# A decoder trunk step: placing the turned rope queries after the finish, not before it, in VectorE's queue

## The reference

```python
def mla_project(xn, pos, w_down, g_q_lora, w_uq, g_kv_lora, g_qn, g_qr, g_kr):
    b, t = xn.shape[:2]
    d = xn @ w_down
    cq = rmsnorm(d[..., :Q_LORA], g_q_lora)
    ...
    q = (cq @ w_uq).reshape(b, t, N_HEADS, QK_NOPE + QK_ROPE)
    cos, sin = rope_cos_sin(pos)
    q_nope = rmsnorm(q[..., :QK_NOPE], g_qn)
    q_rope = apply_rope(rmsnorm(q[..., QK_NOPE:], g_qr), cos[:, None], sin[:, None])
    ...
```

## Time and profile before

| | us |
|---|---|
| median of 3 runs (lowest to highest) | 1959.62 (1959.49 to 1959.9) |
| the profiled execution | 1959.83 |
| its span in the trace | 1958.0 |
| TensorE matmul busy | 1922.3 (98%) |
| VectorE busy | 1073.7 (55%) |
| ScalarE busy | 758.4 (39%) |
| GpSimd busy | 702.9 (36%) |

### The profile page before, as it was taken

One profiled execution on the slowest core, in us unless ns is written; L12 is line 12 of the kernel. 1 busy time (PEld: TensorE's weight loads), 2 busy tenths in 40 slices (PEclk: granted clock), 3 DMA queues, 4 the chain that ended last, 5 costly groups with the idle time before them and its releaser, 6 DMA issues.

```text
span 1958.0 us, 36321 instructions
## 1 busy us (share of the span) xinstructions
PE 1922.3 (98%) x13285; PEld 1845.1 (94%) x13285; DVE 1073.7 (55%) x1844; ACT 758.4 (39%) x1508; POOL 702.9 (36%) x690
## 2 busy tenths in 40 slices
PE   7999999999999999999999999999999999999999
PEld 7886669999999999999999999999889999999998
DVE  3787655565556555468535425428864852542541
ACT  4555555554555555332112112247653211221221
POOL 3340003422223233443333333366545343333331
PEclk9999999999999999999999999999999999999999
DMA  5321001111111110222322322332222222223223
GB/s 148 65 65 36 25 13 43 38 31 50 36 35 34 44 40 16 75 77 85 86 78 84 86 80 81 86 100 73 76 67 83 79 82 86 81 80 86 85 76 91
DMA packets 253078, 131.47 MB, mean 67 GB/s; under 512 B 43073, under 2 KB 250754, under 8 KB 252882
## 3 DMA queue, kind: packets, MB, share of 16 engines
q1 hardware_dynamic: 252514, 128.56, 23.5%
q10 hardware_dynamic: 444, 1.29, 0.2%
HBM read 126.21 MB, written 3.61 MB: 66 GB/s over the span
## 4 chain that ended last, share of the span: by engine, by line
PE 87%; DVE 9%; ACT 2%; issue 2%; DMA 0%; DVEq 0%; POOL 0%; SPq 0%; ACTq 0%; POOLq 0%
PE ps L200 18%; PE ps L203 18%; PE ps L201 18%; PE ps L1220 7%; PE ps L1218 7%; PE ps L1219 7%; PE ps L1248 3%; PE ps L1023 2%; PE ps L998 2%; PE ps L1185 2%; DVE arena L1856 1%; PE ps L232 1%; PE ps L1014 1%; DVE arena L2112 1%; DVE split L1859 1%
## 5 line engine op out<-in xcount | busy, mean ns | idle before, releaser
L200 PE MATMUL ps<-split,whi 128*128 128x288 f32 x3024 | 888.5, 296 | 10.9 <-DVE split L273 4.2
L201 PE MATMUL ps<-split,whi 128*128 128x288 f32 x3024 | 884.8, 295 | 0.0
L203 PE MATMUL ps<-split,wlo 128*128 128x288 f32 x3024 | 855.5, 295 | 0.0
L194 POOL TENSOR_TENSOR wlo<-raw,whi 128x1024 fp32r<-128x1024 f32 x187 | 455.6, 2438 | 614.2 <-ACT whi L171 613.8
L200 PEld LDWEIGHTS ps<-split,whi 128*128 128x128 f32 x3024 | 568.5, 188 | 14.6 <-issue 13.0
L201 PEld LDWEIGHTS ps<-split,whi 128*128 128x128 f32 x3024 | 568.5, 188 | 0.4
L203 PEld LDWEIGHTS ps<-split,wlo 128*128 128x128 f32 x3024 | 555.8, 188 | 0.0
L171 ACT CAST whi<-raw 128x1024 fp32r<-128x1024 f32 x187 | 194.8, 1043 | 373.6 <-DMA raw<-in_ffn_w_up 226.6
L1218 PE MATMUL ps<-split,split 128*128 128x384 f32 x768 | 268.2, 349 | 0.0
L1468 DVE TENSOR_REDUCE ssq<-arena 128x16 f32<-128x1024 f32 x128 | 156.1, 1220 | 186.6 <-ACT arena L1330 186.6
L1220 PE MATMUL ps<-split,split 128*128 128x384 f32 x768 | 257.9, 336 | 0.0
(11 more groups left out here) (282 smaller groups left out, 2095.3 us busy)
## 6 DMA issues: line engine op xcount, KB each, us to landing
raw<-in_ffn_w_up SPq DMA_DIRECT2D x96, 512.0 KB, 3.8
raw<-in_ffn_w_down SPq DMA_DIRECT2D x48, 512.0 KB, 3.9
arena<-in_cache_ckv SPq DMA_DIRECT2D x128, 128.0 KB, 2.0
raw<-in_rec_w_in SPq DMA_DIRECT2D x16, 512.0 KB, 3.9
raw<-in_attn_w_o SPq DMA_DIRECT2D x8, 512.0 KB, 3.9
raw<-in_rec_w_out SPq DMA_DIRECT2D x8, 512.0 KB, 4.1
raw<-in_attn_w_down SPq DMA_DIRECT2D x7, 512.0 KB, 7.6
raw<-in_attn_w_uq SPq DMA_DIRECT2D x48, 64.0 KB, 2.2
```

What stands on the lines that cost most here:

```text
L194: pool.tensor_tensor(wlo[:, t % RING, :], raw[:, t % RING, :], f32(whi[:, t % RING, :]), ALU.subtract).then_inc(w_lo, 1)
L200: pe.matmul(o, wh, a, start=first, stop=False)
L201: pe.matmul(o, wh, b, start=False, stop=False)
L203: mm = pe.matmul(o, wl, a, start=False, stop=last)
```

## The change

In `uq_dve` the call of `uq_place` moves from behind the evacuation to the end of the turn, so that it follows the finish of group p-1.

```diff
@@ -798,8 +798,6 @@
                 uq_evacuate(dve, p)
                 if p == 1:
                     rope_key_turned(dve)
-                if p - 3 in ROPES[:-1]:
-                    uq_place(dve, p - 3)
                 if p == 0:
                     rope_key(dve)
                     down_low(dve, 4)
@@ -810,6 +808,8 @@
                     uq_finish(dve, p - 1)
                 if p - 2 in ROPES:
                     uq_sin(dve, p - 2)
+                if p - 3 in ROPES[:-1]:
+                    uq_place(dve, p - 3)
```

## The result

The changed kernel takes 1975.14 us (median of 4 runs, 1972.96 to 1975.63), against 1959.76 us before on the same chip. The ratio is 1.0073 with a 95% interval of 1.0062 to 1.0085, so it is slower by 12 to 17 us. In the comparisons further down two executions ran at a lower granted clock throughout (one of the kernel before, 2350.82 us at 0.752, and one of turn7, 2060.19 us at 0.946); ratios and intervals leave them out, and the medians move by under 0.2 us with them. The forecast was 1971.8 us in a range of 1964.5 to 1976.0. The profiled execution took 1975.19 us, its span is 1973.3: 15.3 us above the span before.

What follows compares the result with a forecast made beforehand. The prediction took TensorE to bound the kernel (87% of the chain), VectorE's order mattering only where TensorE waits for it. Its terms 2.1 + 7.3 + 1.6 + 1.2 = +12.2 us gave a median of 1971.8 us, range 1964.5 to 1976.0.

Steps and rivals of the forecast that it cites:

- Turn 4, +2.1: Query projection, turn 4: finish(3) waits for the Exp, evacuation(5) and product(6) come 2.1 us later; TensorE stalls 3.0 us.
- Turn 7, rotation earlier, sum(8) +1.5 with a stall of 3.1: Turn 7: rotation(6) starts 1.6 us earlier, but evacuation(8) 1.7 later; sum(8), held by sine(6), starts 1.5 later.
- Turn 9, +7.3 with the 1.5 of turn 8: Turn 9: placement(6) meets two GpSimd subtractions, delaying evacuation(10); product(11) starts 7.3 us later, sum(8)'s 1.5 included.
- The stall of 5.6 us before product(11): Turn 9: TensorE has nothing to do from about 128.8 and stands 5.6 us until product(11).
- The clock, 1.6 + 1.2 = 2.8: Lower granted clock behind stalls: +1.6 us behind the 5.6 us stall, +1.2 for one of the two shorter ones.
- The coin for the two shorter stalls: Stalls of 3.0 and 3.1 us: even odds each of lowering the clock, costing 1.4 or about 1.0; one counted.
- the most for one drop: Limit for one clock drop, from the trace before: 3.9 us of work at half speed cost 1.9 us.
- rival (d): Forecast with other clock outcomes: no stall lowers it, 1969; all do, 1973.5; longer low clock, up to 1976; no separate chance.
- The shift behind the stage: Turns 10 and 11, the value stage and later loads shift rigidly; DMAs cost nothing, a late one a microsecond or two.
- (a): Rival, turn 9: placement(6) does not meet the subtractions, product(11) +2.9 instead of 7.3; +6.2, 1965.8 us; 8%.
- (b): Rival, not slower: finishing earlier pays, rotation(6) 1.6 us earlier, evacuations not delayed; 1958.0 us; 7% in all.
- (c): Rival: only turn 4's +2.1 stays, turns 7 to 9 hide in TensorE's products; 1961.7 us, no change; 5%.

Runs made afterwards that it cites:

- turn7: Kernel before with only placement(4) moved behind finish(6), in turn 7; 1963.46 us, ratio 1.0016.
- sine_first: Changed kernel with sine(6) put ahead of finish(7) in turn 8; 1972.80 us, ratio 1.0059.
- pool_after: Changed kernel with GpSimd waiting for placement(6) before the low parts of the value weights; 1966.85 us, ratio 1.0031.
- turn9_pool: Kernel before with only placement(6) moved behind finish(8), and GpSimd waiting for it before the value weights' low parts; 1962.50 us, ratio 1.0010.
- warm3: Changed kernel with 6, 6 and 9 extra unread matmuls on TensorE ahead of product(6), sum(8) and product(11); 1969.49 us, ratio 1.0048.
- pool_early: Kernel before with GpSimd waiting for finish(3) before the low part of one weight tile, in turn 4; 1960.35 us, ratio 0.9996.
- turn4: Kernel before with only placement(1) moved behind finish(3), in turn 4; 1964.65 us, ratio 1.0021.

## Why the prediction was right, and which term was too small

**Turn 4, +2.1.** Right. The finish waited 2.06 us (2.0 predicted), the placement ended 101.59, and evacuation(5) comes 9.68 us behind evacuation(4) (91.94 to 101.62) instead of 7.65 (92.29 to 99.94): +2.0. TensorE's stall was 3.00 us, the 3.0 of the text.

**Turn 7, rotation earlier, sum(8) +1.5 with a stall of 3.1.** Right in each step. Evacuation(8) came 8.40 us behind evacuation(7) (112.62 to 121.02), before 6.75 (109.38 to 116.13): +1.65 for the 1.7. The stall was 3.06. That the sine holds sum(8) is shown by sine_first.

**Turn 9, +7.3 with the 1.5 of turn 8.** Right as a mechanism: placement(6) lasted 7.20 us for the "about 7.5" (133.45 - 126.0) of the text, and pool_after and turn9_pool show that GpSimd's two subtractions stretch it. Together with turn 4 the sum had 9.4, and warm3, the kernel without the clock's part, measured 9.2. Evacuation(10) stands at 137.65, 2.0 us behind the 135.6 that the prediction gave without any clock cost. That is the clock's 1.6 us of product(6) and 1.1 of sum(8), below, less a start that is 0.35 earlier and a placement 0.25 shorter.

**The stall of 5.6 us before product(11)** was 3.65. Sum(8), the transposes and product(10) ran slow behind the stall before sum(8) and filled the rest; sum(9) was at 132.90, 7.8 us behind sum(8) in place of 5.1. The prediction had said that product(10)'s slowness has slack, and had not carried it into the length of the next stall.

**The clock, 1.6 + 1.2 = 2.8.** This is the term that was too small: 5.3 us in the stage. The coin for the two shorter stalls was counted once, and both fell: product(6) cost 4.79 - 3.23 = 1.6 us (1.4 said), sum(8) 1.1 (1.0 said). Behind the stall of 3.65 us the low level lasted through all of product(11), 5.90 - 3.24 = 2.7 us for the 1.6 taken and beyond the 1.9 that was called the most for one drop. The three add up to 5.4, the 5.3 of the comparison with warm3. That it is the clock, and not something else slow on TensorE, is shown by warm3.

The step that set the 1.9 was a reading of the first drop in the trace before. The prediction took the 3.9 us from the stall's end at 19.10 to about 23.0 for what one drop can cost. But the clock had fallen inside that stall; the windows from which this is seen stand ahead of those in the earlier trace rows:

```profile
16.00:18.00 2.00, 0.00 (x0) 0.00 (x0) 1.30 (x4) 1.21 (x2) 2.00 (x4) 0.54 1.09 320
18.00:20.00 2.00, 0.90 (x4) 0.93 (x5) 2.00 (x3) 2.00 (x4) 0.34 (x1) 0.50 1.19 268
```

At 0.54 on average in 16 to 18 it was low from about 16.2, so for 6.8 us in all, of which 2.9 fell into the stall and cost nothing. Behind product(11)'s stall it was low for 6.8 us as well (137.7 to 144.5), but only 0.9 of them, up to 138.55, lay in the stall. The low stretch was no longer than the one before; more of it lay under work.

With all clock outcomes at their bound the prediction's own sum was 2.1 + 7.3 + 4.8 = 14.2, 1974.0 us against the profiled execution's 1959.83. The result of 1975.14 lies above that. It is in the range only because rival (d) had put the upper end at 1976, for a low level longer than either row shows, and no row gave that figure. The mechanism of each place was right; that the range held was in part luck.

**The shift behind the stage.** Predicted as rigid; 1.2 us were added, and they come from one place near the end. The trace before has its second drop at 1418 to 1422 us and none at 1440 to 1444, where TensorE waited 2.7 us for VectorE's L2157. After, the same wait is 3.0 us, 13.8 us later, and behind it the clock is low. Two windows behind the wait, before and, under it, after:

```profile
1442.00:1444.00 2.00, 2.00 (x18) 1.95 (x17) 0.00 (x0) 0.00 (x0) 1.57 (x1) 1.00 0.00 0
```

```profile
1456.00:1458.00 2.00, 2.00 (x11) 2.00 (x10) 0.00 (x0) 0.00 (x0) 1.33 (x1) 0.50 0.00 0
```

VectorE's last row ahead of L2157 and its next row behind it, which waits for TensorE, before and, under it, after:

```profile
1438.68 0.75 DVE L2153 TENSOR_TENSOR arena<-arena 128x576 f32<-128x576 f32 x1
...
1444.77 1.22 DVE L2210 COPY arena<-ps 36x1024 f32<-36x1024 f32 x1 [3.77 <-PE ps L2205]
```

```profile
1452.48 0.75 DVE L2153 TENSOR_TENSOR arena<-arena 128x576 f32<-128x576 f32 x1
...
1460.15 1.22 DVE L2210 COPY arena<-ps 36x1024 f32<-36x1024 f32 x1 [5.34 <-PE ps L2205]
```

From one to the other it is 6.1 us before and 7.7 after: 1.6 us, where the shift had been 13.8 us. Between the stage's end, at 14.1, and there it had lost 0.3. The drop of before at 1418, which the changed kernel does not have, moved nothing: VectorE's rows are 13.8 us later on both sides of it. Nearly the same stall keeps the clock once and loses it once. A shift of 14 us is not needed for that: pool_early, which is 0.8 us ahead of before at this place, lost the clock there behind a wait of 2.45 us. What decides it, no run here shows. The four executions of the changed kernel seem to differ in the same way: 1972.96 us came with a mean granted clock of 0.996, and 1975.10 to 1975.63 with 0.993 or 0.994, but only one of them has a trace.

**The rivals.** (a), no meeting in turn 9, was 1965.8; pool_after, which makes it so, measured 1966.85, +6.4 over before for the +6.2 of the text, so the rival was well priced and did not happen. (b) and (c) are out by turn7 and by the stall before sum(8). Of (d)'s clock outcomes the one with all stalls lowering the clock, 1973.5, came true. What was measured above it lies in product(11) and in the drop near the end.

## What to carry to other kernels

Work that waits for nothing, placed ahead of work that waits for another engine, covers that wait; moved behind it, it does not merely swap places but makes the next release later, by the wait that is uncovered (2.06 us in turn 4) and by whatever it now meets. Ask of each moved operation which instructions of GpSimd lie in its new stretch, if both its inputs are in SBUF: in turn 9 two subtractions turned 3.04 us of additions into 7.2. And price a stall of TensorE of about 3 us or more with the slow matmuls behind it: here that was 5.3 us on 9.2. Read how long a drop lasts from the whole stretch of windows in which the clock is low, the stall's own included, because another stall can leave more of it under work.

## What the runs showed of the hardware that was not expected

Behind a stall of 3.65 us all 5.9 us of product(11) ran at 0.50, where 3.9 us had done so behind the first stall of the trace before; the low stretches are 6.8 us long both times. Stalls of 2.9 to 3.1 us were followed by the low level in the changed kernel, turn4, turn7, pool_after and sine_first. But the length of a stall alone does not sort them: one of 2.7 us in the trace before kept the clock, and one of 2.45 in pool_early (before L200 at 1439.70) and one of 2.36 in sine_first (before product(10), 129.71) did not. And when VectorE's additions and GpSimd's subtractions both had work queued, they alternated one whole instruction each; neither got two in a row, so that the length of a placement could be summed to 0.3 us.
